# A hybrid mixer and a sparse-attention block: value products of 64-wide heads with the values as weights on two column halves, and the output gate transposed in place of the output

## What is computed

```python
qb = _rope(_heads(qb, N_HEADS_B, HEAD_DIM_B)).reshape(B, S, N_KV_B, GROUP_B, HEAD_DIM_B)
o_b = _banded_attention(qb, _rope(_heads(kb, N_KV_B, HEAD_DIM_B)), _heads(vb, N_KV_B, HEAD_DIM_B),
                        WIN_B, sink=sinks[l].reshape(N_KV_B, GROUP_B))
y_b = o_b.reshape(B, S, WIDTH_B) * jax.nn.silu(zb)

x = x + jnp.concatenate([y_a, y_b], axis=-1) @ w_out[l]
return _rmsnorm(x, final_g)
```

## Time and profile before

| | before |
|---|---|
| median of 3 runs | 1242.67 us (1242.46 to 1242.71) |
| span of the profiled execution | 1240.9 us |
| time of the profiled execution beside its span | not given apart; the runs' median lies 1.8 us above the span |
| PE busy | 1218.7 us (98%), 6566 matmul records |
| DVE busy | 748.4 us (60%) |
| ACT busy | 611.1 us (49%) |
| DMA | 224 MB, mean 181 GB/s |

### The profile page before, as it was taken

How to read it: one execution, slowest core, us unless ns; L and a number is a source line. 1 busy time by engine, 2 the same in 40 slices (tenths; PEclk the granted TensorE clock), 3 DMA queues, 4 the chain that set the end, 5 groups by cost and what they waited for, 6 DMA issues and landing times.

```text
span 1240.9 us, 16520 instructions
## 1 busy us (share of the span) xinstructions
PE 1218.7 (98%) x6566; PEld 1022.1 (82%) x6566; DVE 748.4 (60%) x1008; ACT 611.1 (49%) x898; POOL 95.7 (8%) x129
## 2 busy tenths in 40 slices
PE   8899999999999999999999999999999999999997
PEld 8788888888878888888888888788897778888886
DVE  5668885665576656556455555667565646565654
ACT  5566454544424556444444444564444445466443
POOL 0010000179300000000000000000000000000000
PEclk9999999999999999999999999999999999999999
DMA  8646555576644544655666585466544656464662
GB/s 258 210 140 192 165 182 159 145 214 186 184 142 131 172 129 142 215 189 171 209 181 202 190 296 199 154 208 201 168 138 151 204 170 204 125 218 163 207 206 100
DMA packets 141101, 224.00 MB, mean 181 GB/s; under 512 B 10097, under 2 KB 60849, under 8 KB 140001
## 3 DMA queue, kind: packets, MB, share of 16 engines
q1 hardware_dynamic: 138576, 212.25, 54.6%
q0 software_dynamic: 2128, 9.64, 2.2%
q10 hardware_dynamic: 320, 1.06, 0.2%
HBM read 218.20 MB, written 4.72 MB: 180 GB/s over the span
## 4 chain that ended last, share of the span: by engine, by line
PE 90%; DVE 4%; ACT 3%; issue 1%; DMA 1%; POOL 0%; SPq 0%; POOLq 0%; ACTq 0%
PE acc L1941 62%; PE acc L1920 9%; PE acc L1922 5%; PE aux L1812 3%; PE aux L2186 2%; PE acc L1873 2%; DVE lo_w L1283 1%; PE aux L2162 1%; PE acc L1932 1%; ACT hi_w L902 1%; PE aux L1992 1%; DVE cv L1397 1%; PE aux L2052 1%; DMA x_in<-in_x 0%; PE aux L2155 0%
## 5 line engine op out<-in xcount | busy, mean ns | idle before, releaser
L1283 DVE TENSOR_TENSOR lo_w<-raw_w,hi_w 128x1024 fp32r<-128x1024 f32 x379 | 462.4, 1230 | 346.5 <-ACT hi_w L902 345.1
L902 ACT ACTIVATE hi_w<-raw_w 128x1024 fp32r<-128x1024 f32 x379 | 394.7, 1057 | 267.8 <-PE acc L1941 218.8
L1941 PE MATMUL acc<-hi_w,h_both 128*128 128x512 f32 (+1 forms) x1632 | 520.2, 391 | 1.2 <-DVE lo_w L1283 0.8
L1941 PEld LDWEIGHTS acc<-hi_w,h_both 128*128 128x128 f32 x1632 | 304.7, 188 | 65.6 <-issue 3.9
L1941 PE MATMUL acc<-lo_w,h_both 128*128 128x512 f32 (+1 forms) x816 | 314.6, 385 | 0.0
L1920 PE MATMUL acc<-h_both,hi_w 128*128 128x512 f32 x576 | 204.5, 399 | 2.4 <-DVE lo_w L1283 2.4
L1941 PEld LDWEIGHTS acc<-lo_w,h_both 128*128 128x128 f32 x816 | 153.6, 188 | 28.1
L1922 PE MATMUL acc<-h_both,lo_w 128*128 128x256 f32 x576 | 160.8, 279 | 0.0
L1920 PEld LDWEIGHTS acc<-h_both,hi_w 128*128 128x128 f32 x576 | 108.2, 188 | 28.3 <-DVE lo_w L1283 1.6
L1922 PEld LDWEIGHTS acc<-h_both,lo_w 128*128 128x128 f32 x576 | 108.6, 189 | 0.1
L1941 PE MATMUL acc<-hi_w,m_hi 128*128 128x512 f32 x224 | 87.5, 390 | 0.0
(11 more groups left out here) (348 smaller groups left out, 1246.4 us busy)
## 6 DMA issues: line engine op xcount, KB each, us to landing
raw_w<-in_w_in SPq DMA_DIRECT2D x283, 512.0 KB, 3.8
raw_w<-in_w_out SPq DMA_DIRECT2D x64, 512.0 KB, 4.8
raw_w<-in_w_branch_a SPq DMA_DIRECT2D x16, 512.0 KB, 4.6
raw_w<-in_w_branch_b SPq DMA_DIRECT2D x16, 512.0 KB, 4.7
raw_w<-in_cmp_k_w SPq DMA_DIRECT2D x8, 512.0 KB, 4.3
raw_w<-in_cmp_v_w SPq DMA_DIRECT2D x8, 512.0 KB, 4.9
x_in<-in_x SPq DMA_DIRECT2D x8, 256.0 KB, 8.4
x<-in_x POOLq DMA_DIRECT2D x1, 2048.0 KB, 9.6
```

The source lines that it names most:

```text
L902: act.activation(hi_w[slot][:, 0:n], raw_w[no % RAW_SLOTS][:, 0:n], ACT.Copy).then_inc(*hi_ready.event(no))
L1283: dve.tensor_tensor(lo_w[slot][:, 0:n], raw_w[no % RAW_SLOTS][:, 0:n], hi_w[slot][:, 0:n].bitcast(F32), ALU.subtract).then_inc(*lo_ready.e ...
L1941: i = pe.matmul(to[:, t, 0:group.cols], x[at], w[:, k], start=first and k == 0 and m == 0, stop=last and k == n - 1 and m == 2)
```

## The change

For the 64-wide heads the product with the values is turned round. The values of one key tile (128 keys x 64) are the weights now, and the transposed probabilities stream: 256 columns, which are two heads of 128 tokens. Even heads use the left 64 columns of the array and write partitions 0 to 63, odd heads use the right 64 columns and write partitions 64 to 127. So the result has channels on the partitions, as the last product needs it, and isn't divided by the denominator. VectorE copies it to `ob_t`.

The division goes to the gate. The reciprocals are kept in `b_rden` (`small` grows from 400 to 432 columns). `y_gate(n)` for n = 2, 3 multiplies silu(z) in `z2` by them. `flip("y", n, t)` then transposes this gate, VectorE multiplies it in PSUM by `ob_t` into a new tile `y_t`, and hi and lo parts are made from `y_t`. For n = 0, 1 nothing changes.

```diff
@@ ScalarE
             def flip(name, n, t):
                 b = flip_bank(name, n, t)
-                act.wait_ge(*flip_filled.after(name, n, t))
                 hi = LHS[name][0]
-                act.activation(hi[:, quad(n), t * P:(t + 1) * P],
-                               aux[:, b].rearrange("p (k c) -> p k c", k=QUAD), ACT.Copy).then_inc(
+                if gated_flip(name, n):
+                    act.wait_ge(*dve_did.after("y_t", n, t))
+                    source = y_t[t][:]
+                else:
+                    act.wait_ge(*flip_filled.after(name, n, t))
+                    source = aux[:, b].rearrange("p (k c) -> p k c", k=QUAD)
+                act.activation(hi[:, quad(n), t * P:(t + 1) * P], source, ACT.Copy).then_inc(
                     *flip_hi.event(name, n, t))
@@ VectorE
             def flip(name, n, t):
                 b = flip_bank(name, n, t)
-                dve.wait_ge(*flip_hi.after(name, n, t))
                 hi, lo = LHS[name]
                 at = (slice(None), quad(n), slice(t * P, (t + 1) * P))
-                dve.tensor_tensor(lo[at], aux[:, b].rearrange("p (k c) -> p k c", k=QUAD), hi[at].bitcast(F32),
-                                  ALU.subtract).then_inc(*flip_lo.event(name, n, t))
+                source = aux[:, b].rearrange("p (k c) -> p k c", k=QUAD)
+                if gated_flip(name, n):
+
+                    dve.wait_ge(*flip_filled.after(name, n, t))
+                    dve.wait_ge(*dve_did.after("att", "b", 2 * n - 3, 1))
+                    dve.tensor_tensor(y_t[t][:], source, ob_t[:, quad(n - 2), t * P:(t + 1) * P], ALU.mult).then_inc(
+                        *dve_did.event("y_t", n, t))
+                    source = y_t[t][:]
+                dve.wait_ge(*flip_hi.after(name, n, t))
+                dve.tensor_tensor(lo[at], source, hi[at].bitcast(F32), ALU.subtract).then_inc(
+                    *flip_lo.event(name, n, t))
...
                     dve.wait_ge(*pe_did.after("att", kind, h, t, 4))
-                    w = 64 if kind == "b" else P
-                    o = aux[:, 2, 0:QUAD * w].rearrange("p (i c) -> p i c", c=w)
+                    if kind == "b":
+                        dve.tensor_copy(ob_t[:, 2 * h:2 * h + 2, t * P:(t + 1) * P],
+                                        aux[:, 2, 0:2 * P].rearrange("p (j c) -> p j c", c=P)).then_inc(
+                            *dve_did.event("att", kind, h, t))
+                        return
+                    o = aux[:, 2].rearrange("p (i c) -> p i c", c=P)
...
+                gate = z2[n - 2][:].rearrange("p t (i c) -> p t i c", c=64)
+                r = tiles(b_rden, 16)[:, :, 8 * (n - 2):8 * (n - 1)].unsqueeze(3).broadcast_to([P, NT, 8, 64])
+                dve.tensor_tensor(gate, gate, r, ALU.mult).then_inc(*flip_source.event("y", n))
@@ TensorE
                 b = flip_bank(name, n, t)
-                take(b, (flip_hi, name, n, t), (flip_lo, name, n, t))
+                if gated_flip(name, n):
+                    take(b, (dve_did, "y_t", n, t))
+                else:
+                    take(b, (flip_hi, name, n, t), (flip_lo, name, n, t))
...
-                    w = 64 if kind == "b" else P
-                    for i in range(QUAD):
+                    if kind == "b":
+
                         for b in range(t + 1):
-                            if kind == "m":
-                                v = m_v[:, b, h * QUAD + i]
-                            elif kind == "b":
-                                v = vb[:, b, h // 2]
-                            else:
-                                v = v2["v" + kind][:, b, h]
-                            last = pe.matmul(aux[:, 2, i * w:(i + 1) * w], att_p[:, b, i * P:(i + 1) * P], v,
-                                             start=b == 0, stop=b == t)
+                            p_t = att_p[:, b].rearrange("p (j r c) -> p r j c", r=2, c=P)
+                            for r in range(2):
+                                last = pe.matmul(
+                                    aux[64 * r:64 * (r + 1), 2, 0:2 * P].rearrange("p (j c) -> p j c", c=P),
+                                    vb[:, b, h // 2], p_t[:, r], start=b == 0, stop=b == t)
```

More of the change, by code:

```diff
@@ L449, in build @@
         gnorm_w = place("gnorm_w", [P, P], F32)
-        small = place("small", [P, 400], F32)
+        small = place("small", [P, 432], F32)
         half = place("half", [P, 16], F32)
@@ L458, in bit @@
             top[0] += n
-            assert top[0] <= 400
+            assert top[0] <= 432
             return small[:, top[0] - n:top[0]]
@@ L471, in build @@
         mx, nmx, den, rden, esink = (bit(2 * QUAD) for _ in range(5))
+        b_rden = bit(NT * 16)
         cmx, cden, crden = bit(HEADS), bit(HEADS), bit(HEADS)
@@ L548, in build @@
         oa_tok = arena("oa_tok", [P, NT, HEADS * P], F32, 60)
-        ob_tok = arena("ob_tok", [P, NT, 16 * 64], F32, 68)
+        ob_t = arena("ob_t", [P, HEADS, SEQ], F32, 68)
+        y_t = [arena(f"y_t{t}", [P, QUAD, P], F32, 104 + 2 * t) for t in range(NT)]
         cmp_rows = arena("cmp_rows", [P, 256], F32, 32)
@@ L611, in flip_bank, with gated_flip @@
             return {"oa": 3 * t, "ob": 3, "y": t}.get(name, (2 * n + t) % AUX)
+        def gated_flip(name, n):
+            return name == "y" and n >= 2
         def h2_flipped(k, t):
@@ L1559, in att @@
                     if kind == "b":
+                        r = b_rden[:, t * 16 + h * QUAD:t * 16 + (h + 1) * QUAD]
+                    if kind == "b":
                         link(dve.tensor_tensor(d, d, esink[:, 0:QUAD], ALU.add))
@@ L1577, in att @@
                         return
-                    to = oa_tok if kind in "sw" else ob_tok
-                    to = to[:, t, h * QUAD * w:(h + 1) * QUAD * w].rearrange("p (i c) -> p i c", c=w)
+                    to = oa_tok[:, t, h * QUAD * P:(h + 1) * QUAD * P].rearrange("p (i c) -> p i c", c=P)
                     if kind == "w":
@@ L1583, in att @@
                     else:
-                        last = dve.tensor_tensor(to, o, over_cols(r, w), ALU.mult)
+                        last = dve.tensor_tensor(to, o, over_cols(r), ALU.mult)
                     last.then_inc(*dve_did.event("att", kind, h, t))
@@ L1737, in y_gate @@
                 dve.wait_ge(*dve_did.after(*(("catt", 1) if n < 2 else ("att", "b", 2 * n - 3, 1))))
-                tok = (oa_tok, ob_tok)[n // 2][:, :, n % 2 * COLS:(n % 2 + 1) * COLS]
-                dve.tensor_tensor(tok, tok, z2[n % 2][:], ALU.mult).then_inc(*flip_source.event("y", n))
+                if n < 2:
+                    tok = oa_tok[:, :, n * COLS:(n + 1) * COLS]
+                    dve.tensor_tensor(tok, tok, z2[n][:], ALU.mult).then_inc(*flip_source.event("y", n))
+                    return
+                gate = z2[n - 2][:].rearrange("p t (i c) -> p t i c", c=64)
+                r = tiles(b_rden, 16)[:, :, 8 * (n - 2):8 * (n - 1)].unsqueeze(3).broadcast_to([P, NT, 8, 64])
+                dve.tensor_tensor(gate, gate, r, ALU.mult).then_inc(*flip_source.event("y", n))
             def y2_out(c):
@@ L1954, in flip @@
                     s = merged[:, t]
+                elif n < 2:
+                    s = oa_tok[:, t, n * COLS:(n + 1) * COLS]
                 else:
-                    s = (oa_tok, ob_tok)[n // 2][:, t, n % 2 * COLS:(n % 2 + 1) * COLS]
+                    s = z2[n - 2][:, t]
                 for i in range(QUAD):
@@ L2176, in att @@
                         pe.wait_ge(*act_did.after("values", {"s": "ksv", "w": "kwv", "b": "kvb"}[kind]))
-                    w = 64 if kind == "b" else P
-                    for i in range(QUAD):
+                    if kind == "b":
                         for b in range(t + 1):
-                            if kind == "m":
-                                v = m_v[:, b, h * QUAD + i]
-                            elif kind == "b":
-                                v = vb[:, b, h // 2]
-                            else:
-                                v = v2["v" + kind][:, b, h]
-                            last = pe.matmul(aux[:, 2, i * w:(i + 1) * w], att_p[:, b, i * P:(i + 1) * P], v,
-                                             start=b == 0, stop=b == t)
+                            p_t = att_p[:, b].rearrange("p (j r c) -> p r j c", r=2, c=P)
[3 more added lines that the diff above has]
+                                    vb[:, b, h // 2], p_t[:, r], start=b == 0, stop=b == t)
+                    else:
+                        for i in range(QUAD):
+                            for b in range(t + 1):
+                                v = m_v[:, b, h * QUAD + i] if kind == "m" else v2["v" + kind][:, b, h]
+                                last = pe.matmul(aux[:, 2, i * P:(i + 1) * P], att_p[:, b, i * P:(i + 1) * P], v,
+                                                 start=b == 0, stop=b == t)
                 else:
```

## The result

| | before | after |
|---|---|---|
| median, runs side by side | 1242.67 us (1241.12 to 1244.27, 13 runs) | 1245.08 us (1243.97 to 1246.62, 13 runs) |
| ratio | | 1.002, 95% interval 1.0013 to 1.0027 |
| profiled execution: own time, span | not given, 1240.9 us | 1246.62 us, 1244.8 us |

The changed kernel is 2.4 us slower. The forecast was 1238.8 us, with a range that ended at 1240.8.

The account below looks back on a forecast made before the run. TensorE, busy for 98% of the span, was taken as the bound. Value products save 3.96 us, less 0.1 charged at y 3: 3.9 us off, span 1237.0 plus an unchanged 1.8 gives 1238.8 us, range 1237.6 to 1240.8.

Parts of the forecast that it names:

- What the value products take: TensorE's value products of the 64-wide heads, second block: 11.2 us before, shorter once column halves run side by side.
- (h, 0): Value-product stretch of att("b", h, 0, 4): 4 matmuls become 2 of 256 columns, forecast at 0.61 us.
- (h, 1): Value-product stretch of att("b", h, 1, 4): 8 matmuls become 4 of 256 columns, forecast at 1.02 us.
- The price of the array's division: Switching TensorE's tiling costs 0.08 us more for each of four value-product stretches starting straight after a large product.
- What reaches the end: Value-product savings that shorten the span: seven of the eight stretches, 3.96 us in sum.
- (1,0)'s saving: 0.43 us at att("b", 1, 0, 4), left out: it only lengthens TensorE's 0.82 us wait for lo_w.
- The charge at y 3: Longer flip chain before the last product's next weight splits just fits (1162.0 against 1162.15): 0.1 us charged, bounds 0 to 0.4.
- TensorE's waking: 0.1 us from lo_w done at 1161.9 to TensorE's start on the k = 8 piece, after y 3's flips.
- The sum: 3.96 - 0.1 = 3.9 us off the span of 1240.9: span 1237.0, time 1238.8, 0.31% faster.
- The slower one: Turned value products: halves don't overlap and each pass shows 0.12 us for new weights, 4.7 us more, 1247.4; chance 0.06.
- the early savings are eaten: Between 955 and 1000 us ScalarE and VectorE set the pace; 2.5 us stay after the charge, 1240.2; chance 0.12.
- The signs named for being wrong: In the timeline of after: records of a (h, 0) starting 0.2 us apart one by one, or new lo_w waits.

Follow-up runs that it names:

- the first experiment: Changed kernel with small back at 400 columns and b_rden in a tile of its own behind all others: 1238.66 us, 0.9971 of the kernel before.
- The padded kernel: Changed kernel with small still at 432 columns and 384 bytes more ahead of the tiles behind it: 1238.1 us, 0.9969 of the kernel before.

## Why the prediction was wrong

**What the value products take.** Right. 0.61 us was forecast for a (h, 0) and 1.02 for a (h, 1); the rows show 0.58 and 1.02. The two rows of before that bounded them, scores on halves of the rows and compression products on parts of the columns, held.

**The price of the array's division.** Right: 0.08 forecast, 0.32 - 0.23 = 0.09 measured.

**What reaches the end.** Right. From the rows, before less after: 0.46 at (0,0), 0.91, 0.82, 0.93 - 0.58 - 0.09 = 0.26 twice, 1.82 - 1.02 - 0.09 = 0.71, 1.70 - 1.01 - 0.09 = 0.60: 4.0 us, where 3.96 was forecast. (1,0)'s saving went into the wait for lo_w behind it, which the forecast put at 1.2 to 1.3 us. Timeline of after, beside the earlier trace rows:

```profile
985.07 2.35 DVE L1293 TENSOR_TENSOR lo_w<-raw_w,hi_w 128x1024 fp32r<-128x1024 f32 x2
...
986.44 0.47 PE L1970 MATMUL acc<-hi_w,h_both 128*128 128x512 f32 x1 [1.27 <-DVE lo_w L1293]
```

**The charge at y 3.** Right. It is read best without the slower products, in the first experiment, beside the earlier trace rows:

```profile
1152.67 0.69 DVE L1305 TENSOR_TENSOR y_t<-aux,ob_t 128x512 f32<-128x512 f32 x1 [3.50 <-PE aux L1841]
...
1155.93 3.89 ACT L908 ACTIVATE hi_w<-raw_w 128x1024 fp32r<-128x1024 f32 x4
...
1157.01 4.63 DVE L1293 TENSOR_TENSOR lo_w<-raw_w,hi_w 128x1024 fp32r<-128x1024 f32 x4 [0.26 <-ACT hi_w L908]
...
1157.02 0.39 PE L1970 MATMUL acc<-hi_w,m_hi 128*128 128x512 f32 x1
...
1158.38 0.47 PE L1970 MATMUL acc<-hi_w,m_hi 128*128 128x512 f32 x1
1158.69 0.40 PE L1970 MATMUL acc<-lo_w,m_hi 128*128 128x512 f32 x1
```

From the first reader of the turned blocks to the next hi_w it was 1157.42 - 1156.45 = 0.97 us; it is 1155.93 - 1152.67 = 3.26, that is 2.3 later, which is the forecast's figure. The first of the four lo_w, 1.23 us long, is done at 1158.23, 5.56 us behind the multiply's start, where the forecast had 1161.9 - 1156.45 = 5.45. The piece starts at 1158.38, 0.15 later; the forecast put TensorE's waking at 0.1, for which it showed no row. The first step is 1158.69 - 1158.38 = 0.31 where others are 0.23: 0.08 us, against 0.1 charged.

**The sum, the step that failed.** "3.96 - 0.1 = 3.9 us. The span is 1240.9 us" takes it that all work outside the places that the change touches keeps its length. The line that grows `small` was in view as a size and not as a move of all tiles behind it. The term that it put at nothing is what the 1152 matmuls with weights behind `small` pay for their new distance. The turned products bring 3.9 us (the first experiment, 1238.66 against 1242.55; forecast 1238.8). The distance takes 6.3 (after against the first experiment, each compared with before on its own chip), which makes the 2.4 measured. That these two add up shows nothing, since the second is the difference of the same runs. The distance has two measures of its own, though: the old kernel pays 7.1 us for the same 128 bytes (5.3 to 8.8 by the interval), and 1152 x 6 ns are 6.9. With them the changed kernel would be 3.0 to 3.2 us slower; the difference from 2.4 is within that interval.

That the first experiment lies only 0.1 us from the forecast is luck in part: its interval allows a saving of 2.2 to 4.8 us. The rows above carry the 3.9 better than the time does.

**The rivals.** None was this one. The slower one had the new passes fail to overlap, which the 1.02 us of the (h, 1) rule out; that the early savings are eaten fails on (0,0) and (0,1). The signs named for being wrong, records of a (h, 0) 0.2 us apart or new waits for lo_w, are both absent, and the forecast was wrong all the same. A list of signs has to hold the untouched groups' mean durations too.

**A part of the profile that isn't the change.** In after's profiled execution the clock fell once, near the start (columns: busy us and count of PE, PEld, DVE, ACT, POOL, granted clock, DMA share, GB/s):

```profile
40.00:44.00 4.00, 1.82 (x11) 1.32 (x9) 1.43 (x3) 3.97 (x6) 0.89 (x2) 1.00 0.49 142
44.00:48.00 4.00, 3.55 (x11) 3.07 (x12) 3.80 (x6) 0.27 (x1) 0.00 (x0) 0.57 0.71 202
48.00:52.00 4.00, 4.00 (x24) 3.44 (x24) 3.28 (x7) 2.97 (x6) 0.00 (x0) 1.00 0.84 234
```

In the 4 us ahead of it TensorE was busy for 1.82. At 0.57, near the lower of the two levels, 1.2 GHz, these four can cost at most 4 x 0.43 = 1.7 us, an estimate. The mean clock of this execution, 0.998, is that of others of its kernel too, which took 1244.18 to 1245.64 us, so the dip doesn't by itself make it the slowest. The padded kernel, whose median is the lowest of all, shows the same dip in its profiled execution:

```profile
44.00:48.00 4.00, 4.00 (x15) 3.35 (x14) 3.69 (x4) 1.41 (x4) 0.00 (x0) 0.59 0.68 182
```

So it isn't what makes the changed kernel slower. What sets it off wasn't tried.

## What to carry to other kernels

Treat every change of a tile's size as a move of all tiles behind it. For the matmuls that make up the time work out the weights' address less the stream's, and its remainder modulo 256 bytes; put small new tiles behind the large ones, or pad, to keep it. Then measure, since one group here (`h_both` streaming past weights from `hi_w`) didn't respond. When a result misses, first compare the mean duration of groups that the change leaves alone: 390 against 396 ns in one row says more here than all waits together. Ask of a small expected gain, too, what a change of a few ns in the thousand largest instructions would do to it: it was 3.9 us against 1152 x 6 ns.

## What was unexpected

- **Place of the weights.** A 512-column fp32 matmul with 128 x 128 weights starts every 0.227 us with weights and stream 0 bytes apart (six steps in the first experiment's timeline, 1157.02 to 1158.38). In after, 128 apart, it is (1189.00 - 1187.83) / 5 = 0.234, by this timeline:

```profile
1187.83 0.40 PE L1970 MATMUL acc<-hi_w,m_hi 128*128 128x512 f32 x1
...
1189.00 0.39 PE L1970 MATMUL acc<-hi_w,m_lo 128*128 128x512 f32 x1
```

  By the groups' means it is about 6 ns more at 32, 64 and 128 bytes and 2 at 192. Moving both by 128 bytes does nothing (1241.32 against 1242.55 us). The Trainium skill, "TensorE: Matmul & The Clock Gate", part 2 (Step-by-step: what each phase is for), says that two independent SBUF read ports feed the weight load and the stream, and that loading the next weights takes no read bandwidth from the running matmul. By that the distance would cost nothing; the runs show 6.3 to 7.1 us of it at 32 to 128 bytes. That the two reads meet somewhere in the memory is a guess from the dependence on the distance; no run shows where. Only multiples of 32 bytes and six distances besides 0 were tried, and 384 with the buffers moved apart.
- **Halves pair by themselves.** Column halves overlap whether they alternate in the program or come two by two (1.02 us both).
